# Stores of activations and gates issued from ScalarE's queue instead of SyncE's

## The reference, cut to what matters

```
q = (ht @ w_q).reshape(T, PEER_HEADS, 2, PEER_DKEY // 2)          # T = 512 tokens, 8 heads
s = einsum('thpd,pnd->thpn', q, sub_keys)                         # 2 x 128 keys a head
... the best 16 of 128 x 128 pairs of keys a head: idx; g = softmax of their scores
act = gelu(einsum('cd,chkd->chk', xc, u_experts[ic]))
out = einsum('chk,chkd->cd', gc * act, v_experts[ic])             # 16384 experts of 1024
```

## Time and profile before

| | |
|---|---|
| median of 3 runs | 2100.16 us (2097.12 to 2106.31) |
| profiled execution, its own time | 2099.87 us |
| its span, first to last instruction | 2098.0 us |
| busy: PE, DVE, ACT, POOL | 90%, 76%, 35%, 38% of the span |
| `phase_experts` in the span | about 803 to 1551 us: 80 tiles to 1242, 48 tiles from there |
| stores that the change moves | 64 of 384 KB, 12 of 2048 KB |

### The profile page before, as it was taken

The page is one execution under the profiler, slowest core; times in us unless marked ns, Lnnn a source line. Parts: engine busy times, 40 slices in busy tenths (PEclk is TensorE's granted clock), DMA queues, the critical chain, the costliest instruction groups (busy, mean ns, idle before and its releaser), DMA issues. The chain is left out here.

```text
span 2098.0 us, 28277 instructions
## 1 busy us (share of the span) xinstructions
PE 1880.0 (90%) x10096; PEld 1630.3 (78%) x10096; DVE 1587.1 (76%) x2260; ACT 729.5 (35%) x970; POOL 789.7 (38%) x487
## 2 busy tenths in 40 slices
PE   4999789999899798978787878899969999999998
PEld 4888666777679688878777778888858888888886
DVE  6444365553446588989999889999958888887887
ACT  3222234443323222322222245555534333333331
POOL 0000293000140003579687876666632332333320
PEclk7999989999999899999999999999989999999999
DMA  8754123333661523679999989999989999999991
GB/s 284 261 180 140 45 76 91 91 91 105 214 228 41 103 61 83 156 213 286 243 277 248 257 222 287 276 277 275 285 298 385 381 386 370 357 357 354 368 349 74
DMA packets 312737, 475.96 MB, mean 227 GB/s; under 512 B 16426, under 2 KB 239451, under 8 KB 311132
## 3 DMA queue, kind: packets, MB, share of 16 engines
q1 hardware_dynamic: 275804, 340.89, 54.3%
q0 software_dynamic: 36864, 134.23, 18.9%
HBM read 413.71 MB, written 60.82 MB: 226 GB/s over the span
## 5 line engine op out<-in xcount | busy, mean ns | idle before, releaser
L117 PE MATMUL u_s<-h_hi,u_hi 128*128 128x384 f32 x1024 | 357.2, 349 | 72.9 <-POOL u_lo L1502 67.4
L1502 POOL TENSOR_TENSOR u_lo<-u_ut,u_hi 128x1024 fp32r<-128x1024 f32 x127 | 320.4, 2523 | 175.7 <-ACT u_hi L1526 175.0
L119 PE MATMUL u_s<-h_hi,u_lo 128*128 128x384 f32 x1024 | 346.5, 338 | 0.0
L118 PE MATMUL u_s<-h_lo,u_hi 128*128 128x384 f32 x1024 | 346.5, 338 | 0.0
L117 PE MATMUL v_o<-v_v_hi,v_w_hi 128*128 128x512 f32 x768 | 299.9, 391 | 16.8 <-DVE v_w_lo L1938 15.6
L118 PE MATMUL v_o<-v_v_lo,v_w_hi 128*128 128x512 f32 x768 | 299.5, 390 | 0.0
L119 PE MATMUL v_o<-v_v_hi,v_w_lo 128*128 128x512 f32 x768 | 299.5, 390 | 0.0
L117 PEld LDWEIGHTS u_s<-h_hi,u_hi 128*128 128x128 f32 x1024 | 195.2, 191 | 91.7 <-issue 40.3
L1877 ACT ACTIVATE v_v_hi<-v_raw 128x1024 fp32r<-128x1024 f32 x128 | 127.5, 1051 | 338.0 <-PE v_o L119 275.6
L1583 DVE CUSTOM_DVE_ANT_0 rows_buf<-rows_buf,u_ht 128x1024 f32<-128x1024 f32 x128 | 215.9, 1697 | 12.5 <-DMA rows_buf<-in_u_experts_dram,few_idx 12.5
L1904 DVE TENSOR_TENSOR v_v_lo<-v_raw,v_v_hi 128x1024 fp32r<-128x1024 f32 x128 | 149.5, 1220 | 86.2 <-ACT v_v_hi L1877 85.9
(11 more groups left out here) (308 smaller groups left out, 3648.9 us busy)
## 6 DMA issues: line engine op xcount, KB each, us to landing
u_raw<-in_u_experts_dram SPq DMA_DIRECT2D x256, 256.0 KB, 6.4
v_raw<-in_v_experts_dram SPq DMA_DIRECT2D x128, 512.0 KB, 5.8
expert_acts<-u_ao SPq DMA_DIRECT2D x64, 384.0 KB, 4.2
expert_gates<-u_gs SPq DMA_DIRECT2D x12, 2048.0 KB, 7.5
v_gt<-expert_gates SPq DMA_DIRECT2D x32, 768.0 KB, 14.7
w_in_raw<-in_w_in_dram SPq DMA_DIRECT2D x17, 1024.0 KB, 5.5
proj_ada<-in_w_ada_dram SPq DMA_DIRECT2D x8, 2048.0 KB, 8.4
gate_w_raw<-in_w_in_dram SPq DMA_DIRECT2D x32, 512.0 KB, 4.0
```

What stands on the lines that cost most here:

```text
L117: nc.tensor.matmul(out, w[0], x[0], start=first, stop=False)
L118: nc.tensor.matmul(out, w[0], x[1], start=False, stop=False)
L119: return nc.tensor.matmul(out, w[1], x[0], start=False, stop=last)
L1502: nc.gpsimd.tensor_tensor(lo[j][:, :, :], ut[j][:, :, :], hi[j][:, :, :].bitcast(F32), ALU.subtract).then_inc(sem["lo_ok"], 1)
```

## The change: what it does

`store` and `gates_out` are moved from SP's program to ACT's. They wait for the same counts as before (`act_ok`, `g_ok`), now on ACT. A pair is stored right behind the Gelu of its odd tile. A chunk of gates is stored behind the Gelu of the fourth tile of the chunk, ahead of the pair's store. Before, SP issued the gates as soon as their last copy was done, which is ahead of that tile's product. SP's program keeps the loads; two waits (`a_out0`, `a_out1`) are added ahead of the first read of `expert_acts`.

```
-            def store(n, j):
-                sp.wait_ge(sem["act_ok"], 2 * n + 2)
-                sp.dma_start(au[n], ao[j][:, :, :]).then_inc(sem[f"a_out{j}"], 16)
-            def gates_out(c, j):
-                sp.wait_ge(sem["g_ok"], (c + 1) * (CH // 4))
-                sp.dma_start(gates[c], gs[j][:, :, :]).then_inc(sem[f"g_out{j}"], 16)
...
-                    store(2 * i + j, j)
...
-                    if x % 2:
-                        gates_out(2 * i + x // 2, x // 2)
-                    store(n, x % 2)
...
+                        sp.wait_ge(sem["a_out0"], 32)
+                        sp.wait_ge(sem["a_out1"], 16)
...
+            def store(n, j):
+                act.wait_ge(sem["act_ok"], 2 * n + 2)
+                act.dma_start(au[n], ao[j][:, :, :]).then_inc(sem[f"a_out{j}"], 16)
+
+            def gates_out(c, j):
+                act.wait_ge(sem["g_ok"], (c + 1) * (CH // 4))
+                act.dma_start(gates[c], gs[j][:, :, :]).then_inc(sem[f"g_out{j}"], 16)
...
+                    if j % 2:
+                        store(2 * i + j // 2, j // 2)
...
+                    if x % 4 == 3:
+                        gates_out(2 * i + x // 4, x // 4)
+                    if x % 2:
+                        store(PLAIN // 2 + i * (UNROLL // 2) + x // 2, x // 2 % 2)
```

## The result

| | before | after |
|---|---|---|
| median of 12 runs | 2103.72 us | 2113.89 us |
| ratio to before, 95% interval | | 1.0048 [1.0025, 1.0071] |
| profiled execution, its own time | 2099.87 us | 2103.41 us |
| span | 2098.0 us | 2101.6 us |

The change makes the kernel 0.5% slower: 10.1 us, with an interval from 5.3 to 14.9. The forecast was 22.5 us above the profiled execution that it started from (2099.87). The profiled execution of after is the fastest of its twelve, so its span alone would mislead; where it matters I use the ratios.

What follows compares the result with a forecast made beforehand. In the last 48 tiles a two-tile loop through DVE, PE, ACT and POOL of 12.70 us without slack was taken as the bound; 2099.87 + 18.3 (last 48 tiles) + 1 (first 80) + 3.2 (phase end) = 2122.4 us, range 2104 to 2142.

Steps and rivals of the forecast that it cites:

- The pair's store ahead of the rounding: Last 48 tiles: ACT's issue delays the next rounding by 0.58 or 0.73 us a pair, 15.8 us in all.
- the gates': Last 48 tiles: 11 gates' issues on ACT ahead of a rounding cost 4.6 us, of which 2.5 were taken.
- POOL's wait for ACT grows: Sign expected in the changed profile; before, POOL waits 93.8 us for ACT between 1255 and 1551 us.
- The port: DVE in a two-port mode and POOL contend for ports; whichever issues first blocks the other for its whole instruction.
- That each further issue adds its length: Last 48 tiles: each issue ahead of a rounding delays it, 0.58 or 0.73 us for a pair's store, 0.42 for gates.
- relief for the gates: Last 48 tiles: behind both stores `u_match` goes first at the port, giving part of the gates' 4.6 us back.
- The end of the phase: Gates leave behind the last Gelu, 3.2 us later, all on the path: +3.2 us, bounds +2 and +6.
- The first 80 tiles: Issues cost 2.9 and 1 us, shorter `u_raw` waits give 3 back: +1 us, bounds -17.3 and +29.
- third rival: ACT's issue waits for SP's where a store meets a load, 1 us for each of 24 pairs: 2147; chance 0.10.
- The port's order: First rival, last 48 tiles: `u_match` of odd tiles gets ahead of POOL, so they cost nothing: 2104; chance 0.13.
- Faster by earlier loads: Second rival: issue doesn't delay rounding, DVE's 17.3 us of DMA waits in first 80 tiles mostly go: 2086; chance 0.07.
- ACT behind SP: The third rival: ACT's store issue waits for SP's load issue, 1 us a pair; chance 0.10.

Runs made afterwards that it cites:

- run 2: Kernel before, with only the stores of the last 48 tiles (pairs and gates) moved to ACT: 2123.08 us, ratio 1.0082.
- run 3: Changed kernel, all stores on ACT, but each pair's store issued behind the next rounding and the gates ahead of the Gelu: 2092.32 us, ratio 0.9954.
- run 6: Changed kernel, with each pair's store in the last 48 tiles issued as two halves ahead of the rounding: 2115.07 us, ratio 1.0037.
- run 4: Kernel before, all stores on SP, each pair's store one load later in SP's queue, ACT untouched: 2092.21 us, ratio 0.9946.
- run 9: Changed kernel, but SP again waits for the pair's Gelus behind each load and issues 512 bytes in the store's place: 2119.76 us, ratio 1.0083.
- run 1: Kernel before, with only the pair stores of the first 80 tiles moved to ACT: 2096.49 us, ratio 0.9965.
- run 10: As run 4, with ACT's rounding ahead of the Gelu in the last 48 tiles alone: 2084.47 us, ratio 0.9919.
- run 7: As run 4, with ACT's rounding of tile t+2 ahead of the Gelu of tile t: 2096.65 us, ratio 0.9957.

## Why the prediction was right or wrong, point by point

- *The pair's store ahead of the rounding, 15.8 us, and the gates', 2.5 after what comes back.* Right in mechanism, and the sum in size: forecast 18.3 us for 48 tiles, which is 16.0 for 42; measured 16.2, a pair of tiles in 13.52 us. Runs 2 and 3 show it: the loss comes and goes with the issue's place alone. That the sum fits to 0.3 us is in part luck. The pair's store costs more than forecast, 0.61 us in the written-out turns and 0.81 in the loop for 0.58 and 0.73, together 17.2 us for 15.8. The gates' store costs less, since its issue runs beside the Gelu that it follows: the 23 steps are 19.8 us longer than before in all, so the gates have 2.6 of it, not 4.6. Some 1 us of the 19.8 comes back, not 2.1.
- *The sign "POOL's wait for ACT grows".* It did not: 93.8 us before, 89.2 after, between 1255 and 1551 us. What grew is the time that POOL is held inside its subtractions (18.6 us in the whole kernel), where no view of waits shows it.
- *The port.* The rule that the forecast cites is for VectorE in a two-port mode, and no row shows a mode. The rows show that `u_match`, `u_hot` and the dot product, each with two inputs, shut out POOL's subtraction and are shut out by it, and that the transposition, with one, is not.
- *That each further issue adds its length.* The forecast used this for the first issue and halved it for the second, and run 6 shows where it ends: with the rounding 1.93 us behind the Gelu the port's order has turned and next to nothing is added (1.1 us in 42 tiles for 24 more issues). The forecast's relief for the gates (2.1 us) was this effect; it came at four of ten, and the way to it was half known.
- *The end of the phase, 3.2 us.* Right; measured 2.4. The two transfers together land faster than when the second was issued 3.3 us after the first.
- *The first 80 tiles, +1.* This is the step that failed, as a term wrongly sized: 2.9 + 1 us of cost against 3 us off the waits for `u_raw`. From the ratios: 10.1 - 18.6 - 2.4 = -10.9 us. Run 4, which has the gain of the loads alone, measures -11.4, of which 0.4 are the phase's end (5.1 us instead of 5.5). In the profiles of both kernels some 2 to 3 us of the difference lie ahead of the phase. What is left is about 8 us for the loads, against the 3 of the forecast. That it is the loads, and not ACT's later rounding, is shown by run 4, where ACT's program is untouched, and borne out by run 9, where held loads lose most of it again; its size is known to some 5 us only, the half width of the intervals. The forecast saw the load behind the store's wait in SP's queue, and priced it by DVE's direct wait, 4.8 us. The cost that it set against this is smaller than the intervals: -7.4 us in run 1 with the issue ahead of the rounding, -9.7 in run 3 with it behind, in all. A part of it can be seen where the stages join, from tile 76 to tile 84: 53.6 us in after and 53.7 in run 1, 50.2 before, 51.9 in run 3.
- *The sum.* 22.5 forecast, 10.1 measured. The difference is this one term but for half a us, and of it 2 to 3 us lie outside of the phase by the profiles. The range held it. The third rival's time, 2147, is 24 us above the forecast's 2122.4, so 2146.
- *The rivals.* The port's order does turn, but as a ceiling (run 6). Faster by earlier loads was the right thing to fear: its mechanism is worth about 8 us, and it lost only because the last part pays more; its condition, that ACT's issue doesn't hold up the rounding, did not come. ACT behind SP: 59 ns at most, in the 13 stores that met a load.

What stays open is why the loads give about 8 us when DVE's waits for `u_raw` are 5, and where the 2 to 3 us ahead of the phase come from. The waits were shorter in each kernel with free loads except run 6 (7.0), and in run 9 they returned with the loss. A load that comes late also moves all that DVE does behind it, and the meetings at the port with it; the dot products' time differs by 36 us between the profiles (195.9 in run 10 to 231.7 in run 2). With one or two profiles a kernel the two can't be told apart.

## What to carry to other kernels

An engine at 35% can stand in a loop without slack: before an issue is moved to it, sum the loop's starts from one instance to the next, and if the sum is the period, put the issue where that engine waits anyway. Here one place costs 16 us and the other, two instructions on, nothing. On the queue that is relieved, ask which transfer stood behind the wait of another: reordering SP's own queue got the whole gain with no second queue. And look where a difference of two profiles begins: here 2 to 3 us of it arise ahead of the code that was changed. And where DVE and POOL take turns, an instruction's length that varies is the wait to look for, since no view lists it.

## What the runs showed of the hardware

- A DMA issue holds ACT's sequencer for 352 ns (gates) or 378 (a pair), and the next activation waits for its end: from Gelu to rounding 0.39 us without it, 1.01 with a pair's store in written-out code and 1.19 to 1.21 in a loop with addresses from registers. Where such an issue met one on SP, it took up to 437 ns.
- DVE's `u_match`, `u_hot` and dot product and POOL's subtraction exclude each other for whole instructions: 1.18, 1.76, 1.22 and 2.40 us alone, and 2.25 to 3.42, 3.85, 3.02 and 3.47 when they come second. So DVE and POOL do not meet through semaphores alone. DVE's transposition runs beside POOL's subtraction at its full speed: 1.24 us at 1486.61 in run 7's kernel and at 1510.26.
- From issue to landing, medians of the pages of after and before: the pair's store takes 6.5 us from ACT and 4.2 from SP, the gates 9.6 and 7.5, and `u_raw` 5.5 and 6.4. No run separates what sets these times.
